# Layer 0's border in another order, two key tiles beside an attention's first items, and weight chunks split inside the work ahead of them

## The chip, the cores and the metric

One core of a Trainium2 chip runs the whole program in one launch. The metric is device time in microseconds. The kernel before took 1628.4 us (median of three runs, 1627.59 to 1629.45).

## What is computed

Two blocks of two layers each, fp32, width D = 1024, one sequence x of 256 tokens; the second block has a context ctx of 256 tokens beside it. The part that the change touches, cut:

```python
# first block: h = layer_norm(DN_ALPHA*h + mixer(h)), a pooling mixer, then a dilated attention whose
# keys and values come from h @ w_kv; its result h is the x of the second block.
def rms_norm(x, g): return x * rsqrt(mean(x*x) + EPS) * g
for l in range(2):                          # second block
    sh1, sc1, g1, sh2, sc2, g2 = split(silu(c) @ w_mod[l] + b_mod[l], 6)     # for x, and the same for ctx
    h_x, h_c = [rms_norm(v, norm_g[l, 0]) * (1 + sc1) + sh1 for v in (x, ctx)]
    if l == 0:   # even mixer, on x and ctx
        qa, ka, va, qb, kb, vb = split_cols(h @ w_in[l], EVEN_SPLITS)
        qa, ka = rms_norm(qa, qk_g[0]), rms_norm(ka, qk_g[1])                # 8 query heads, 2 key heads of 64
        # x's q and k get a rotary embedding; x attends to ctx and x, ctx to ctx
        o_a = softmax(qa @ ka.T) @ va
        lam = exp(sum(lam_p[0]*lam_p[1])) - exp(sum(lam_p[2]*lam_p[3])) + lam0
        o_b = rms_norm((softmax(qb1 @ kb1.T) - lam * softmax(qb2 @ kb2.T)) @ vb, subln_g) * (1 - lam0)
    else:        # odd mixer: windowed attention C with a sink, neighbourhood attention D with the bias rpb
        o_a, o_b = windowed_attend(...), neighborhood_attend(..., rpb)
    x = x + g1 * rms_norm(concat(o_a, o_b) @ w_out[l], norm_g[l, 1])
    h2 = rms_norm(x, norm_g[l, 2]) * (1 + sc2) + sh2
    x = x + g2 * rms_norm(square(relu(h2 @ w_mlp_in[l])) @ w_mlp_out[l], norm_g[l, 3])
    # ctx gets the same two updates in layer 0
```

## The kernel before

**Weights.** All weights come as one stream of 210 chunks of 1 MB (128 x 2048) through three `raw` slots, issued by SP (SyncE). A matrix product is made of three fp32r products (`mm3`, L548 to L550): high half by high, low by high, high by low. So each chunk is split: ACT (ScalarE) copies its high half into `whi` (`split_hi`, L1014), DVE (VectorE) subtracts it into `wlo` (`split_lo`, L1024). There are four split slots, and ACT waits before chunk w until the unit of chunk w − 4 is `used` up by PE (TensorE). A unit is one weight block, such as q2, k2, v2 (the projections of the second block), out, in and out of the MLP. `split_to(name)` on ACT and on DVE splits all chunks up to the end of that unit and ahead of it, as far as slots allow; with a second argument 0 only up to its end; `last_split` (L996) works out which chunk that is. The features (activations, token or feature on the partitions) are split in the same way, into `fhi` by ACT (L1069) and `flo` by DVE or POOL (L1556, L2243).

**Order.** Each engine's program is written out by hand. An instruction gives a label by `did(...)`, and another engine waits by `after(...)`; an engine goes strictly in order, so what stands behind a waiting instruction waits with it. PSUM's banks are handed out in turn by `job(...)` on PE, which waits until the bank's last user has been `read` by ACT or DVE.

**Tiles.** Token tiles 0 and 1 are x, 2 and 3 are ctx, each of 128 tokens. `by_token` (L562) projects tiles of tokens with a unit; q2 is 512 columns wide, k2 256 (two key heads and two value heads). `turn_normed` transposes normed tiles into features (L600), with `modulate` (DVE or POOL) making h * (1 + scale) + shift on the way.

**The border between the blocks.** The last projection of the first block is unit outb, in two halves of one unit each, for x's tiles 0 and 1. DVE adds the residual (`add_residual`), takes `statistics` and `moments`, ACT takes the `root` of the variance, DVE the `gain_shift` (layer norm). Then ACT squares the tile (`squares`) and takes the root for the second block's rms norm (`stream_root`, L1325), and DVE norms it (`normed`, L1929 to L1937). The ctx tiles need only the latter. ACT's list is at L1355 to L1373, DVE's at L2097 to L2140, PE's in the branch for l == 0 near L919. After it, PE goes q2 of ctx, k2 of ctx, transposes of x, q2 of x, heads of ctx turned, k2 of x, attention.

**Attentions.** Each attention is a list of items; an item is the scores of one head and one tile of queries (L682, L690), DVE's maximum (L1764), ACT's exponential, PE's transposes of the probabilities (L724) and the product with the values (L752). Work that has no part in them is set between the items as side steps, pairs of (item, step): `side_steps_pairs` for the second attention of layer 0, the differential one (16 items), `side_steps_halves` for its first. Every engine runs through the same list in `attend` (PE L755, ACT L1237, DVE L1850) and does its share of a step. Head norms are made by `head_squares` (ACT, L1390), `head_sums` (DVE, L2020 to L2029), `head_roots`, `head_scaled`, and `turn_heads` (PE).

**The first block's attention** has DVE's two instructions for lam (L1923 and L1924) in front of its items; they wait for ACT's exponential of the sums (L1297).

**MLP of layer 0.** `hidden(0, j)` on ACT and `square_hidden` on DVE make the hidden features of in-unit j, for the first two units with ctx and x apart; `mlp_out` on PE multiplies with out-unit j later. Between layers stand `residual` (L1967), `stream_root` and `normed` again.

**Layer 1.** `split_to(("k2", 1, 0), 0)`, the wait for the DMAs of the odd mixer's tables (`loads["odd"]`, L2121) and `modulate(("n1", 1, 1), ...)` follow each other on DVE. POOL adds the rpb rows to the column mask, one instruction for each of the bias loads (L2298).

## Time and profile before

| | |
|---|---|
| median of three runs | 1628.4 us (1627.59 to 1629.45) |
| the profiled execution: its own time, its span | 1627.03 us, 1625.2 us |
| PE busy (matmuls; weight loads beside them) | 1531.4 us, 94% of the span (1307.4 us, 80%) |
| DVE busy | 872.8 us, 54% |
| ACT busy | 677.1 us, 42% |
| POOL busy | 152.6 us, 9% |
| TensorE clock granted, mean | 0.977 of full speed |
| DMA | 233.89 MB, mean 144 GB/s |

The span is the time from the first to the last instruction of one execution. PE busy is the union of its matmuls; its ends are modelled, so a busy PE need not be at its peak. Under half clock, the same matmuls take about twice the time and PE counts as busy all the same.

### The profile page before, as it was taken

What the parts mean: (1) busy time and instruction counts of PE and PEld (TensorE: products, weight loads), DVE (VectorE), ACT (ScalarE), POOL (GpSimd) and SP (SyncE); (2) the same over time, 40 slices, a digit from 0 to 9 for tenths busy, and PEclk for the clock granted to TensorE, in tenths of its full rate; (3) what the DMA queues carried; (4) which work ended last, traced back from release to release, by engine and by line L of the source; (5) the groups of instructions that cost most, each with busy time, mean ns of one, the idle gap of its engine ahead of it and who ended that gap; (6) DMA issues with size and microseconds to landing.
All of it is one profiled execution on the core that took longest, in us unless ns stands there. A gap on an engine that the chain in (4) does not pass through costs nothing.

```text
span 1625.2 us, 24158 instructions
## 1 busy us (share of the span) xinstructions
PE 1531.4 (94%) x9546; PEld 1307.4 (80%) x9546; DVE 872.8 (54%) x1505; ACT 677.1 (42%) x1096; POOL 152.6 (9%) x119
## 2 busy tenths in 40 slices
PE   7999899999999979998998999999998999979998
PEld 7998798999997756785797777777786777779887
DVE  6786654545546765347574343333457455655444
ACT  5454344544435335336454122232235335544443
POOL 2100310000000110000013001111002020020110
PEclk9999999999999979999999999999999999989999
DMA  6455655353536315220231453543512421145451
GB/s 247 173 200 208 231 209 198 138 182 131 182 106 231 135 52 208 104 87 18 78 130 53 156 188 135 195 183 134 201 52 94 134 71 53 69 166 188 175 194 66
DMA packets 43770, 233.89 MB, mean 144 GB/s; under 512 B 13136, under 2 KB 14224, under 8 KB 16784
## 3 DMA queue, kind: packets, MB, share of 16 engines
q1 hardware_dynamic: 31232, 222.38, 36.8%
q10 hardware_dynamic: 12432, 10.01, 2.2%
q8 instruction: 77, 1.26, 0.3%
q14 instruction: 29, 0.24, 0.0%
HBM read 231.29 MB, written 1.08 MB: 143 GB/s over the span
## 4 chain that ended last, share of the span: by engine, by line
PE 84%; DVE 8%; ACT 4%; issue 2%; POOL 1%; DMA 0%; ACTq 0%; DVEq 0%; SPq 0%
PE ps L548 23%; PE ps L550 23%; PE ps L549 23%; PE ps L752 5%; PE ps L638 3%; DVE wlo L1024 3%; PE ps L724 3%; PE ps L690 2%; ACT whi L1014 2%; PE ps L682 1%; PE ps L600 1%; DVE nmax L1764 1%; POOL flo L2243 1%; PE ps L622 1%; ACT fhi L1069 0%
## 5 line engine op out<-in xcount | busy, mean ns | idle before, releaser
L1024 DVE TENSOR_TENSOR wlo<-raw,whi 128x2048 fp32r<-128x2048 f32 x162 | 383.5, 2392 | 282.9 <-ACT whi L1014 282.7
L548 PE MATMUL ps<-fhi,whi 128*128 128x256 f32 (+1 forms) x1280 | 393.3, 307 | 13.6 <-DVE wlo L1024 7.1
L1014 ACT ACTIVATE whi<-raw 128x2048 fp32r<-128x2048 f32 x162 | 304.0, 1906 | 224.3 <-PE ps L550 168.7
L549 PE MATMUL ps<-flo,whi 128*128 128x256 f32 (+1 forms) x1280 | 389.3, 304 | 0.0
L550 PE MATMUL ps<-fhi,wlo 128*128 128x256 f32 (+1 forms) x1280 | 389.3, 304 | 0.0
L548 PEld LDWEIGHTS ps<-fhi,whi 128*128 128x128 f32 x1280 | 247.3, 193 | 37.3 <-issue 9.5
L549 PEld LDWEIGHTS ps<-flo,whi 128*128 128x128 f32 x1280 | 247.2, 193 | 8.9
L550 PEld LDWEIGHTS ps<-fhi,wlo 128*128 128x128 f32 x1280 | 247.0, 193 | 9.0
L548 PE MATMUL ps<-whi,fhi 128*128 128x512 f32 (+1 forms) x592 | 209.6, 354 | 14.3 <-DVE mix L2029 5.4
L549 PE MATMUL ps<-wlo,fhi 128*128 128x512 f32 (+1 forms) x592 | 206.1, 348 | 0.0
L550 PE MATMUL ps<-whi,flo 128*128 128x512 f32 (+1 forms) x592 | 206.1, 348 | 0.0
L548 PE MATMUL ps<-whi,hhi 128*128 128x512 f32 x384 | 153.2, 399 | 7.8 <-issue 7.8
L550 PE MATMUL ps<-whi,hlo 128*128 128x512 f32 x384 | 152.2, 396 | 0.0
L549 PE MATMUL ps<-wlo,hhi 128*128 128x512 f32 x384 | 152.2, 396 | 0.0
L548 PEld LDWEIGHTS ps<-whi,fhi 128*128 128x128 f32 x592 | 114.8, 194 | 33.0 <-issue 6.6
L550 PEld LDWEIGHTS ps<-whi,flo 128*128 128x128 f32 x592 | 114.6, 194 | 13.6
L549 PEld LDWEIGHTS ps<-wlo,fhi 128*128 128x128 f32 x592 | 114.9, 194 | 12.7
L1992 DVE TENSOR_TENSOR htmp<-htmp 128x256 f32<-128x256 f32 (+1 forms) x72 | 47.1, 654 | 116.3 <-ACT htmp L1349 116.3
L2254 POOL TENSOR_TENSOR hlo<-htmp,hhi 128x256 fp32r<-128x256 f32 (+1 forms) x72 | 66.4, 922 | 439.3 <-ACT hhi L1354 439.3
L548 PEld LDWEIGHTS ps<-whi,hhi 128*128 128x128 f32 x384 | 72.5, 189 | 29.1 <-issue 12.1
L550 PEld LDWEIGHTS ps<-whi,hlo 128*128 128x128 f32 x384 | 72.3, 188 | 17.6
L549 PEld LDWEIGHTS ps<-wlo,hhi 128*128 128x128 f32 x384 | 72.5, 189 | 17.0
(238 smaller groups left out, 1784.4 us busy)
## 6 DMA issues: line engine op xcount, KB each, us to landing
raw<-in_wstream SPq DMA_DIRECT2D x210, 1024.0 KB, 5.0
gates<-gated ACTq DMA_DIRECT2D x6, 512.0 KB, 4.3
hx<-in_x SPq DMA_DIRECT2D x1, 1024.0 KB, 5.1
lnrow<-in_ln_g ACTq DMA_DIRECT2D x2, 512.0 KB, 4.1
lnrow<-in_ln_b ACTq DMA_DIRECT2D x2, 512.0 KB, 5.3
hc<-in_ctx ACTq DMA_DIRECT2D x1, 1024.0 KB, 6.0
mix<-in_rpb_rows ACTq DMA_DIRECT2D x4, 256.0 KB, 5.1
hc<-in_rpb_rows ACTq DMA_DIRECT2D x4, 256.0 KB, 3.9
```

The source lines that it names most:

```text
L548: mm(o, lh, rh, start=start, stop=False)
L549: mm(o, lh, rl, start=False, stop=False)
L550: return mm(o, ll, rh, start=False, stop=stop)
L600: ins = nc.tensor.transpose(o[:, c:c + P], src(t)[:, k * P:k * P + P], ident[:, :])
L638: ins = mm(o[at:at + 32, :], condz[:, 2 * k:2 * k + 32], raw[:, c % RAW_SLOTS, base:base + NW], start=k < 4, stop=k >= 4, tile_position=(0 ...
L690: ins = mm(o, QT[l][po:po + DH, tq, q0 + t * P:q0 + t * P + P], KT[l][po:po + DH, tk, k0:k1], start=True, stop=True)
L724: ins = nc.tensor.transpose(o[:, (j - b) * P:(j - b + 1) * P], e[:, i % 3, j * P:j * P + P], ident[:, :])
L752: ins = mm(o[:, 0:dv], p[:, i % 2, j * P:j * P + P], v, start=j == 0, stop=j == kt - 1)
L1014: nc.scalar.activation(whi[:, w % SPLIT_SLOTS, :], raw[:, c % RAW_SLOTS, :], ACT.Copy).then_inc(*did("scalar", ("hi", w)))
L1024: nc.vector.tensor_tensor(wlo[:, w % SPLIT_SLOTS, :], raw[:, c % RAW_SLOTS, :], whi[:, w % SPLIT_SLOTS, :].bitcast(F32), ALU.subtract).the ...
L1992: v.tensor_tensor(h, h, h, ALU.mult).then_inc(*did("vector", ("squared",) + key))
L2254: p.tensor_tensor(hlo[:, j % 2, e, cols], htmp[:, e % 2, cols], hhi[:, j % 2, e, cols].bitcast(F32), ALU.subtract).then_inc(*did("pool", * ...
```

## The change

Eight places are edited. Lambda's two DVE instructions move from the first block's attention to layer 0's border. In the border, ACT's root for ctx comes before the features and weights, chunks for outb and q2 are split as their slots come free, and PE's order becomes k2 of one ctx tile, transposes of x, k2 of the other, q2 of tile 0, heads of ctx, q2 of tile 1. k2 of x's tiles becomes the side step "keys" of items 0 and 1 of the attention that follows; one chunk is split before that attention and one, the step "ahead", at item 2; roots, scalings and turns come one item later. In layer 0's second attention, the transposes of the mixed ctx tiles ("fo") go from items 13 and 14 to 15 and 16. In the MLP, the chunks of out-unit 0 are split between the last two groups of hidden tiles. At the border to layer 1, k2's chunk is split ahead of the norm, the residual has one label for each tile so that ACT squares a tile behind its own, and modulate goes ahead of the wait for the tables. POOL's bias add is made in four quarters.

```diff
--- before.py
+++ after.py
...
@@ -433,7 +433,7 @@
         return None
-    if step[0] in ("chunk", "bias", "mod", "fo", "weights", "roots", "scaled", "turn"):
+    if step[0] in ("chunk", "bias", "mod", "fo", "weights", "roots", "scaled", "turn", "keys", "ahead"):
         return None
...
@@ -447,7 +447,7 @@
-    return [(1, ("v2", 0, 1, 0)), (3, ("v2", 0, 1, 1)), (12, ("weights",))] + [(13 + j // 2, ("fo", j)) for j in range(4)]
+    return [(1, ("v2", 0, 1, 0)), (3, ("v2", 0, 1, 1)), (12, ("weights",))] + [(15 + j // 2, ("fo", j)) for j in range(4)]
...
@@ -463,9 +463,10 @@
-    return [(2, ("roots",)), (3, ("scaled", "q", 0)), (4, ("scaled", "k", 0)), (5, ("scaled", "q", 1)),
-            (6, ("scaled", "k", 1)), (7, ("turn", "q", 0)), (8, ("turn", "k", 0)), (9, ("turn", "q", 1)),
-            (10, ("turn", "k", 1))]
+    return [(0, ("keys", 0)), (1, ("keys", 1)), (3, ("roots",)),
+            (2, ("ahead", PLACE[UNIT["q2", 0, 1].w0] + 1)),
+            (4, ("scaled", "q", 0)), (5, ("scaled", "k", 0)), (6, ("scaled", "q", 1)), (7, ("scaled", "k", 1)),
+            (8, ("turn", "q", 0)), (9, ("turn", "k", 0)), (10, ("turn", "q", 1)), (11, ("turn", "k", 1))]
...
@@ -764,11 +765,15 @@
             for at, step in steps:
-                if step[0] in ("chunk", "bias", "weights", "roots", "scaled"):
+                if step[0] in ("chunk", "bias", "weights", "roots", "scaled", "ahead"):
                     continue
...
                         turn_heads(step[1], 0, [step[2]], 4 if step[1] == "q" else 2)
+                    continue
+                if step[0] == "keys":
+                    if at == i:
+                        by_token(UNIT["k2", 0, 0], ("k2", 0, 0), [step[1]], width=256, first=False, last=step[1] == 1)
                     continue
...
@@ -919,12 +924,13 @@
                 by_token(UNIT["q2", 0, 0], ("q2", 0, 0), (2, 3), feat=("n1", 0, 1), last=False)
-                by_token(UNIT["k2", 0, 0], ("k2", 0, 0), (2, 3), width=256, last=False)
+                by_token(UNIT["k2", 0, 0], ("k2", 0, 0), [2], width=256, last=False)
                 turn_normed(0, 0, 0)
-                by_token(UNIT["q2", 0, 0], ("q2", 0, 0), (0, 1), feat=("n1", 0, 0), first=False)
+                by_token(UNIT["k2", 0, 0], ("k2", 0, 0), [3], width=256, first=False, last=False)
+                by_token(UNIT["q2", 0, 0], ("q2", 0, 0), [0], feat=("n1", 0, 0), first=False, last=False)
                 turn_heads("q", 0, (2, 3), 4)
                 turn_heads("k", 0, (2, 3), 2)
-                by_token(UNIT["k2", 0, 0], ("k2", 0, 0), (0, 1), width=256, first=False)
+                by_token(UNIT["q2", 0, 0], ("q2", 0, 0), [1], first=False)
             else:
...
@@ -1250,6 +1256,12 @@
                     continue
+                if step[0] in ("keys", "ahead"):
+                    if at == i and step[0] == "keys":
+                        head_squares("k", step[1])
+                    elif at == i:
+                        split_hi(act, step[1], st)
+                    continue
                 if at == i and step[0] == "bias":
...
@@ -1323,12 +1335,12 @@
     def stream_root(l, which, group):
-        if which or l:
-            act.wait_ge(*after("resid", *((l, 0) if which else (0, 1)), group))
-        elif group != (2, 3):
+        if not which and not l and group != (2, 3):
             act.wait_ge(*after("ln", 1, group[0]))
...
             for t in group:
+                if which or l:
+                    act.wait_ge(*after("resid", *((l, 0) if which else (0, 1)), t))
                 squares(("sq", l, which, t), t)
...
@@ -1357,17 +1369,18 @@
         squares(("sq", 0, 0, t), t)
+    stream_root(0, 0, (2, 3))
     split_features("fo1", 0)
     split_to(("outb", 0))
-    stream_root(0, 0, (2, 3))
     split_features(("n1", 0, 1), 1, (0, 0))
     for t in range(XT):
-        if t:
-            split_to(("outb", 1))
-            split_to(("k2", 0, 0), 0)
         act.wait_ge(*after("var", 1, t))
         root(rstd[:, t:t + 1], mv[:, t, 1:2], 1, 1, "root", "ln", 1, t)
+        if t == 0:
+            split_to(("outb", 1))
         stream_root(0, 0, (t,))
+        if t == 0:
+            split_to(("k2", 0, 0), 0)
...
@@ -1407,7 +1420,6 @@
             if l == 1:
-                split_to(("k2", 1, 0), 0)
                 split_features(("n1", 1, 1), 1, (1, 0))
...
@@ -1415,14 +1427,12 @@
                     head_squares("k", t)
-                for t in (0, 1):
-                    head_squares("q", t)
+                split_hi(act, PLACE[UNIT["q2", 0, 1].w0], st)
+                head_squares("q", 0)
                 for what in "qk":
...
                         turned(what, 0, t)
-                split_to(("k2", 0, 0))
-                for t in (0, 1):
-                    head_squares("k", t)
+                head_squares("q", 1)
             elif part == 0:
...
@@ -1483,6 +1493,7 @@
             hidden(0, 0, 0)
+            split_to(("out", 0, 0), 0)
             hidden(0, 1, 0)
...
@@ -1500,8 +1511,9 @@
             mixer_root(0, 1, (2, 3))
+            split_to(("k2", 1, 0), 0)
             stream_root(1, 0, (2, 3))
-            act.wait_ge(*after("resid", 0, 1, (2, 3)))
+            act.wait_ge(*after("resid", 0, 1, 3))
             act.wait_ge(*after("split", ("n1", 1, 0), 3))
...
@@ -1866,6 +1878,10 @@
                     low_feature(("fo", 0, 1), 1, step[1])
+                if at == i and step[0] == "keys":
+                    head_sums("k", step[1])
+                if at == i and step[0] == "ahead":
+                    split_lo(step[1], st)
                 if at == i and step[0] == "roots":
...
@@ -1919,10 +1935,6 @@
                                  heads_view(qkg[:, i, 16 * (1 - half):], (0, 2), (32, 2), (1, 16)), ALU.mult))
-    dve.wait_ge(*after("lam exp"))
-    link(v.tensor_tensor(lam[:, 2:3], lam[:, 1:2], lam[:, 0:1], ALU.subtract))
-    link(v.tensor_scalar(lam[:, 3:4], lam[:, 2:3], -LAM0, None, ALU.add))
-
     items = items_first()
...
@@ -1971,7 +1983,7 @@
                 dve.wait_ge(*after("gated half", l, which, t, n))
-            labels = [("resid", l, which, group)] if t == group[-1] else []
+            labels = [("resid", l, which, t)]
             if l and which:
...
@@ -2095,46 +2107,50 @@
         if l == 0:
+            mod_columns(0, 0)
             low_features("fo1", 0)
-            mod_columns(0, 0)
             normed(0, 0, (2, 3))
-            for t in range(XT):
-                if t:
-                    split_to(("outb", 1))
-                else:
-                    split_to(("outb", 0))
-                for n in range(2):
-                    if n == 0:
-                        dve.wait_ge(*after("h1", t))
-                    add_residual("outb", n, t)
-                    statistics("outb", n, t)
-                    if (t, n) == (0, 0):
-                        modulate(("n1", 0, 1), 0, 0, 1)
-                moments(1, t)
-                gain_shift(t)
-                if t:
-                    split_to(("k2", 0, 0), 0)
-                normed(0, 0, (t,))
+            split_to(("outb", 0))
+            dve.wait_ge(*after("h1", 0))
+            add_residual("outb", 0, 0)
+            statistics("outb", 0, 0)
+            modulate(("n1", 0, 1), 0, 0, 1)
+            add_residual("outb", 1, 0)
+            statistics("outb", 1, 0)
+            moments(1, 0)
+            gain_shift(0)
+            dve.wait_ge(*after("h1", 1))
+            add_residual("outb", 0, 1)
+            statistics("outb", 0, 1)
+            split_to(("outb", 1))
+            normed(0, 0, (0,))
+            add_residual("outb", 1, 1)
+            statistics("outb", 1, 1)
+            moments(1, 1)
+            gain_shift(1)
+            split_to(("k2", 0, 0), 0)
+            normed(0, 0, (1,))
+            dve.wait_ge(*after("lam exp"))
+            link(v.tensor_tensor(lam[:, 2:3], lam[:, 1:2], lam[:, 0:1], ALU.subtract))
+            link(v.tensor_scalar(lam[:, 3:4], lam[:, 2:3], -LAM0, None, ALU.add))
             modulate(("n1", 0, 0), 0, 0, 0, before=("n1", 0, 1))
-        else:
+        if l == 1:
+            modulate(("n1", 1, 1), 1, 0, 1)
             dve.wait_ge(loads["odd"], 48)
             link(v.tensor_scalar(nsink[:, :], sinkr[:, :], -1.0, None, ALU.mult))
-        if l == 1:
-            split_to(("k2", 1, 0), 0)
-            modulate(("n1", 1, 1), 1, 0, 1)
         if l == 0:
-            for g in (1, 0):
-                for what in "qk":
-                    for t in (2 * g, 2 * g + 1):
-                        head_sums(what, t)
-                if g:
-                    head_roots(1)
-                    for what in "qk":
-                        for t in (2, 3):
-                            head_scaled(what, t)
+            for what in "qk":
+                for t in (2, 3):
+                    head_sums(what, t)
+            head_roots(1)
+            for what in "qk":
+                for t in (2, 3):
+                    head_scaled(what, t)
+            split_lo(PLACE[UNIT["q2", 0, 1].w0], st)
+            for t in (0, 1):
+                head_sums("q", t)
             dve.wait_ge(loads["late"], 32)
             link(v.tensor_scalar(sublng[:, :], sublng[:, :], 1.0 - LAM0, None, ALU.mult))
-            split_to(("k2", 0, 0))
             items = items_second(0, 0)
...
@@ -2176,6 +2192,7 @@
             square_hidden(0, 0, 0)
+            split_to(("out", 0, 0), 0)
             square_hidden(0, 1, 0)
...
@@ -2203,6 +2220,7 @@
             residual(0, 1, (2, 3))
+            split_to(("k2", 1, 0), 0)
             normed(1, 0, (2, 3))
...
@@ -2295,8 +2313,9 @@
         rows = b.rearrange("p t (h c) -> p (t h) c", c=S)
-        p.tensor_tensor(rows, rows, heads_view(colmask, (0, 8), (1, S)), ALU.add).then_inc(
-            *did("pool", *([("bias",)] if n else [])))
+        for h in range(0, 8, 2):
+            p.tensor_tensor(rows[:, h:h + 2, :], rows[:, h:h + 2, :], heads_view(colmask, (0, 2), (1, S)), ALU.add).then_inc(
+                *did("pool", *([("bias",)] if n and h == 6 else [])))
     low_modulated(("n2", 1, 0), 1, 1, 0)
...
```

## Rows read from the trace of the kernel before

**Rows 1.** The chain of waits that ended last, shares of the span by engine

```profile
PE 84%; DVE 8%; ACT 4%; issue 2%; POOL 1%; DMA 0%; ACTq 0%; DVEq 0%; SPq 0%
```

**Rows 2.** Timeline, first attention: start us, length us, engine, line, operation, [idle before <-releaser]

```profile
265.11 1.56 PE L682 MATMUL ps<-kq 64*128 64x256 f32 x12
...
267.99 0.16 DVE L1923 TENSOR_TENSOR lam<-lam 128x1 f32<-128x1 f32 x1 [5.11 <-ACT lam L1297]
...
275.42 0.58 PE L548 MATMUL ps<-fhi,whi 128*128 128x256 f32 x1 [2.80 <-ACT kq L1213]
```

**Rows 3.** Stretches: window, us, busy of PE, PEld, DVE, ACT, POOL, clock, DMA, GB/s

```profile
275.40:281.60 6.20, 6.18 (x29) 6.18 (x30) 5.78 (x7) 2.69 (x4) 0.00 (x0) 0.51 0.75 280
...
573.80:578.50 4.70, 4.70 (x11) 3.73 (x12) 4.18 (x18) 0.45 (x3) 0.66 (x1) 0.51 0.00 0
...
601.50:609.60 8.10, 7.94 (x35) 3.87 (x35) 5.44 (x22) 3.40 (x13) 0.00 (x0) 0.53 0.51 192
...
889.40:893.00 3.60, 3.60 (x10) 2.86 (x11) 2.06 (x1) 0.97 (x1) 0.00 (x0) 0.58 1.00 403
```

**Rows 4.** Timeline, layer 0's border, first half

```profile
517.54 2.07 ACT L1069 ACTIVATE fhi<-ps 128x512 fp32r<-128x512 f32 x4 [0.93 <-PE ps L600]
...
523.22 1.28 ACT L1143 ACT_TABLE_LOAD   x1
...
527.27 3.55 PE L600 MATMUL ps<-ident,mix 128*128 128x128 f32 x16 [2.54 <-DVE mix L1937]
...
549.45 0.47 PE L548 MATMUL ps<-whi,fhi 128*128 128x512 f32 x1 [2.27 <-issue]
```

**Rows 5.** Timeline, layer 0's border, second half, PE

```profile
560.65 0.36 PE L548 MATMUL ps<-whi,fhi 128*128 128x256 f32 x1
...
566.48 1.91 PE L600 MATMUL ps<-ident,mix 128*128 128x128 f32 x16
...
573.80 0.79 PE L548 MATMUL ps<-whi,fhi 128*128 128x512 f32 x1 [5.42 <-DVE mix L2029]
```

**Rows 6.** Timeline, opening of layer 0's first attention

```profile
587.78 0.69 DVE L2027 TENSOR_REDUCE hss<-mix 128x8 f32<-128x512 f32 x1 [2.64 <-ACT mix L1397]
...
594.10 1.14 PE L690 MATMUL ps<-kT,qT 64*128 64x256 f32 x8
...
596.05 4.49 DVE L1024 TENSOR_TENSOR wlo<-raw,whi 128x2048 fp32r<-128x2048 f32 x2
...
601.53 0.69 PE L724 MATMUL ps<-ident,e 128*128 128x128 f32 x2 [6.30 <-ACT e L1166]
...
610.31 0.70 PE L690 MATMUL ps<-kT,qT 64*128 64x256 f32 x4
```

**Rows 7.** Timeline, end of layer 0's second attention

```profile
768.50 0.87 PE L600 MATMUL ps<-ident,mix 128*128 128x128 f32 x3 [4.63 <-DVE mix L1846]
...
773.79 1.29 DVE L1556 TENSOR_TENSOR flo<-ps,fhi 128x512 fp32r<-128x512 f32 x2 [2.86 <-ACT fhi L1069]
```

**Rows 8.** Timeline, MLP of layer 0, first out-unit

```profile
882.84 5.49 ACT L1014 ACTIVATE whi<-raw 128x2048 fp32r<-128x2048 f32 x3
...
884.76 6.69 DVE L1024 TENSOR_TENSOR wlo<-raw,whi 128x2048 fp32r<-128x2048 f32 x3 [2.28 <-ACT whi L1014]
...
889.36 0.76 PE L548 MATMUL ps<-whi,hhi 128*128 128x512 f32 x1 [7.75 <-issue]
```

**Rows 9.** Timeline, border of layer 1

```profile
1244.65 0.17 DVE L2121 TENSOR_SCALAR nsink<-sinkr 128x8 f32<-128x8 f32 x1 [1.38 <-DMA band<-in_t_band]
...
1247.29 0.46 PE L548 MATMUL ps<-whi,fhi 128*128 128x256 f32 x1 [1.94 <-DVE wlo L1024]
...
1258.52 0.58 PE L548 MATMUL ps<-whi,fhi 128*128 128x256 f32 x1 [3.76 <-DVE e_b L2084]
```

**Rows 10.** Timeline, last attention: POOL's bias add and a DVE instruction beside it

```profile
1323.72 6.09 POOL L2298 TENSOR_TENSOR mix<-mix 128x2048 f32<-128x2048 f32 x1 [69.25 <-DMA hc<-in_rpb_rows]
...
1326.31 3.52 DVE L1799 TENSOR_TENSOR nmax<-nmax,nsink 128x1 f32<-128x1 f32 x1
```

## The prediction

> **What bounds the kernel now.** I began with the chain of waits that ended last: 84% of it is PE [rows 1]. So a microsecond is worth something only where PE stands idle or runs at half clock, and I listed PE's idle stretches of over one microsecond in its timeline. The reader should look at two things in such a row: the number in brackets (how long PE had been idle) and the engine behind the arrow. Beside it stands the granted clock of the stretch behind the gap. It has two levels, 1.00 (2.4 GHz) and 0.50 (1.2 GHz), and after four of the gaps here it was about 0.5 for 3 to 10 us [rows 3], though PE was then busy nearly all the time. So a gap costs its length and something behind it. Eight of the gaps lie where the diff edits: at the first attention's opening, three at layer 0's border, one at the opening of its first attention, one in its second, one in its MLP and three at the border of layer 1.
>
> **The change, part by part.** All times are of the profiled execution: span 1625.2 us, its own time 1627.0, while the median of the three runs is 1628.4, 1.4 above it. I make the sum against 1627.0 and add the 1.4.
>
> *1. Lambda out of the way of the first attention.* The DVE instruction at 267.99 had waited 5.11 us for ACT's exponential of lam, and the first item's maximum stands two short instructions behind it, at 268.4, although its scores ended at 266.67 (265.11 + 1.56) [rows 2]. The two instructions go to layer 0's border, where they cost 0.4 us in DVE's stream before the last modulate. The maximum, the exp and what ACT does behind it (two weight splits, then the copies of k) move up by 1.7. PE's gap of 2.80 at 275.42 is ended by those copies [rows 2], so it shrinks to 1.1. Behind it, the clock was 0.51 for 6.2 us [rows 3]: 3.1 us of full-rate work lost. With so short a gap I expect most of that back, but not for certain. Value 3.6; bounds 1.5 (clock stays down) and 4.5.
>
> *2. Layer 0's border, first half.* PE's gap of 2.54 at 527.27 waited for DVE's normed ctx tiles, and the 16 transposes there took 3.55 us where the same 16 took 1.91 at 566.48 [rows 4, 5]. DVE in turn waited for the root, which ACT ran behind two weight splits, the table load at 523.22 being its first part [rows 4]. Now the root stands directly behind the two squares, near 516.6. That puts 1.28 (load) + 0.3 (root) ahead of the first attention's features; ACT had 0.93 idle before them [rows 4], so PE starts the outb projection 0.65 later and then runs through: 2.54 + 1.64 − 0.65 = 3.5 gained.
> The Trainium skill ("ScalarE: Activation LUTs", What ACT_TABLE_LOAD costs) gives 2.66 us for a switch of sets, a drain of 1.38 included. By it this part would gain 1.4 less. In the trace the load took 1.28 and the root began right behind it; the sum uses that.
> The next gap, 2.27 at 549.45 [rows 4], is q2's weights: ACT split them only behind tile 0's square and root, DVE behind tile 0's norm. Now both split them as soon as the slots are free, ahead of that. By my replay the low half of the first chunk lands 0.4 after PE gets there: 1.9 gained. On the other side, k2's chunk is split between tile 1's statistics and its norm, and by the same replay PE waits 0.4 for it. Together 3.5 + 1.9 − 0.4 = 5.0; bounds 3.0 and 5.8.
>
> *3. Border, second half.* The gap of 5.42 at 573.80 lay between the transposes of x's normed tiles and q2 of tile 0 [rows 5]. From the first transpose (566.48) to 573.80 are 7.3 us, and this chain (modulate on DVE, copy on ACT, low half on POOL, then DVE's first reading of q2's tile 2, which frees the bank) is unchanged. But k2 of tile 3 now stands inside it: two k2 tiles take 566.48 − 560.65 = 5.8 [rows 5], so one fills 2.9, and the gap falls to 2.5. Behind the old gap the clock was 0.51 for 4.7 us [rows 3], 2.3 lost. Behind the 2.54 of part 2 the transposes ran at half rate too [rows 4], so a gap of this size can bring it; I take 1.6 of the 2.3. Value 2.9 + 1.6 = 4.5; bounds 2.9 and 5.2.
>
> *4. Opening of the attention over ctx and x.* Before, all of q2 and k2 came first, then PE stood still for 6.30 us at 601.53 while DVE did the sums of two k2 tiles and 4.49 us of weight splits at 596.05 before the first maximum; the clock then was 0.53 for 8.1 us [rows 3, 6]. From the end of the projections (594.10, where the first scores begin) to the scores of items 6 and 7 (610.31) are 16.2 us [rows 6]. Now k2's x tiles (2 × 2.9) are done by PE at items 0 and 1, one chunk is split before the attention and the other, the step "ahead", at item 2. Replayed with the rows' durations: DVE's sums of q2's tile 1, of four instructions like that at 587.78 [rows 6], follow the projection with ACT's square ahead of them; the first maximum starts 3.7 after it; then DVE and ACT take turns (maximum, exp, squares, sums) for items 0 to 2, and at item 2 ACT splits 1.9 and DVE 2.3, each waiting for the other. The probabilities' copy of item 0 stands behind ACT's split, so PE idles about 4 us there and 1.5 more at item 1's, and reaches the scores of items 6 and 7 some 18.7 after the projections. Of these, 5.8 are work that stood before the 594.1: 16.2 − (18.7 − 5.8) = 3.3 gained at full clock. A gap of 4 will bring half clock again; as its first part falls into waiting, I charge 1.5. Queued behind the added waits are, on DVE, the roots and the maxima of items 3 and later, and on ACT every exp. From item 7 on PE is busy nearly all the time in this attention, and the later roots, scalings and turns (one item later than before) lie beside it. Value 1.8; bounds −3 (the taking of turns longer by two 2.3-us splits) and 3.5.
>
> *5. Second attention of layer 0.* PE waited 4.63 us at 768.50 for the end of DVE's norm of the ctx pairs, as the transposes of the mixed tiles came at item 13 [rows 7]. Worse, they made DVE wait for ACT's copies of them, 2.86 at 773.79 [rows 7], in a stretch where DVE sets the pace. Now they come at items 15 and 16. PE's gap does not go, it waits for item 12's probabilities instead; but DVE no longer idles: by replay, 3.6 us until the last probabilities. Bounds 2.5 and 4.2.
>
> *6. MLP of layer 0.* PE idled 7.75 us at 889.36, at the first product with w_mlp_out. ACT had split nothing until 882.84, behind all 16 half-width hidden tiles, and DVE's low halves came from 884.76 [rows 8]. Now the first two chunks are split before the last four hidden tiles. Their slots are free when PE ends its last product with the first "in" unit, four half-width products of 2.9 (as a k2 tile [rows 5]) before it went idle at 881.6: at 870. ACT and DVE need 3.7 and 4.5 us, done by about 878, before the 881.6. The four hidden tiles come later by up to 5 us, but PE needs them only a unit later. All 7.75 go, and the half clock behind it (0.58 for 3.6 us [rows 3]) gives 1.5 to 2.0 more. Value 9.6; bounds 7.7 and 10.
>
> *7. Border of layer 1.* DVE stood 1.38 at 1244.65 for a DMA, then did k2's low half, and PE waited 1.94 for that at 1247.29; the modulate stood behind both, and PE's 3.76 at 1258.52 hangs on it through the split and DVE's first reading of q2 [rows 9]. Now k2's split is ahead of the norm, the square of each tile follows its own residual, and modulate is ahead of the DMA wait. Modulate moves from 1247.1, behind that low half, to about 1243.8 and so does all behind it: 3.2, with the clock behind the gap unsettled. Value 3.0; bounds 1.5 and 3.5.
>
> *8. POOL's bias adds in quarters.* A DVE instruction of 0.16 us took 3.52 at 1326.31, while POOL's add of 6.09 ran [rows 10]. The quarters shorten such a block, but PE had projections to do meanwhile: 0; bounds −0.3 and 0.5.
> The Trainium skill ("SBUF — State Buffer", Who interferes with whom) says that a DVE instruction with two SBUF inputs and a GpSimd one hold a shared port pair each for its whole length, which these rows agree with. It also lets the loser be POOL. That changes nothing in the sum.
>
> Sum: 3.6 + 5.0 + 4.5 + 1.8 + 3.6 + 9.6 + 3.0 = 31.1. 1627.0 − 31.1 = 1595.9, and with the 1.4, 1597.3.
>
> **The rivals.** *A: the opening eats the border.* DVE and ACT serve items 0 to 3 alone and in turn; if part 4 goes to its bound and the clock stays at half behind parts 1, 3 and 4, 5 + 2 + 1.6 + 1.5 are missing: about 1607. For it speaks that all of the opening's stall was DVE's work even before [rows 6], and that DVE now gets more of it there; against it, that PE has 5.8 us of keys to do there.
> *B: the clock comes back everywhere.* Gains at the upper bounds of 1 to 4 and 6: about 1592.
> *C: nothing much.* The gains would have to be returned by a later bound, weights above all. No gap of PE in the rows is put down to a weight transfer, so little speaks for it: 1626 to 1630.
> *D: slower.* The clock is the one mechanism that can cost this much: with the small gaps spread where there were few large ones, PE could be held at 1.2 GHz through the long products. To undo 31 us it takes 62 us more at half clock than now; with 80 us more, 1637. Against it: in each half-clock stretch PE had been idle just before, and the change leaves fewer such places.
>
> **How the numbers follow.** Forecast as worked out (1591 to 1603): 0.68. A: 0.20. B: 0.08. C: 0.02. D: 0.02. The predicted time is the forecast's, 1597. For 8 in 10, the range takes in nearly all of A and the inner part of B: 1591 to 1609. A measurement here tells about 0.2%, 3.3 us, from no change: faster 0.96, same 0.02, slower 0.02.
>
> **What would show it.** PE's timeline: no gap before the first product with w_mlp_out (part 6); none of over 1 us before the transposes of the ctx tiles and before q2 in the border (part 2); the gap before q2 of tile 0 near 2.5 (part 3); first probabilities' transposes without 6 us before them but a gap of about 4 before item 0's values (part 4); DVE without the 2.86 wait in the second attention (part 5); no wait for lam (part 1); k2 of layer 1 directly behind its transposes (part 7). The prediction is wrong if PE's idle time merely moves to items 0 to 8 of the attention, or if the half-clock stretches grow longer than those they replace.

## The result

The changed kernel takes 1600.8 us (median of four runs, 1599.48 to 1601.32), the kernel before 1628.0 beside it; the ratio is 0.9831, 95% interval 0.9818 to 0.9843. That is 27.2 us less, where 31.1 had been forecast. In the two profiled executions the spans are 1625.2 and 1599.5, 25.7 apart: that of before was 1.0 under its median (1627.0), that of the changed kernel 0.5 above (1601.3).

The page of the changed kernel: its span, the busy rows, and the chain that ended last, by engine [rows 1].

```profile
span 1599.5 us, 24162 instructions
PE 1525.6 (95%) x9546; PEld 1301.0 (81%) x9546; DVE 867.3 (54%) x1505; ACT 677.1 (42%) x1096; POOL 153.8 (10%) x125
...
PE 83%; DVE 10%; ACT 3%; issue 2%; POOL 1%; DMA 0%; ACTq 0%; DVEq 0%; SPq 0%
```

PE does the same 9546 products in 5.8 us less busy time; the rest of the gain is idle time that went. Where it went is read from PE's timeline after, at the places of the prediction (start us, length us, engine, line, operation, [idle before <-releaser]; the lines of the changed file are 1 to 18 higher):

```profile
275.12 0.38 PE L549 MATMUL ps<-fhi,whi 128*128 128x256 f32 x1 [1.21 <-ACT kq L1219]
...
522.13 1.91 PE L601 MATMUL ps<-ident,mix 128*128 128x128 f32 x16
...
540.82 0.47 PE L549 MATMUL ps<-whi,fhi 128*128 128x512 f32 x1 [0.42 <-issue]
...
562.61 0.50 PE L549 MATMUL ps<-whi,fhi 128*128 128x512 f32 x1 [2.67 <-DVE mix L2041]
...
588.58 1.08 PE L753 MATMUL ps<-vv,p 128*128 128x64 f32 x4 [4.08 <-ACT p L1191]
...
592.85 3.64 PE L639 MATMUL ps<-raw,condz 128*32 128x512 f32 x16
597.52 0.70 PE L691 MATMUL ps<-kT,qT 64*128 64x256 f32 x4
...
600.33 0.66 PE L753 MATMUL ps<-vv,p 128*128 128x64 f32 x4 [1.11 <-DVE modrow L1700]
...
758.81 1.12 PE L725 MATMUL ps<-ident,e 128*128 128x128 f32 x4 [4.28 <-DVE e L1824]
...
868.32 0.39 PE L549 MATMUL ps<-whi,hhi 128*128 128x512 f32 x1
...
1220.70 1.94 PE L601 MATMUL ps<-ident,mix 128*128 128x128 f32 x16 [1.53 <-DVE mix L1949]
...
1232.94 0.58 PE L549 MATMUL ps<-whi,fhi 128*128 128x256 f32 x1 [4.55 <-DVE e_b L2096]
```

Against [rows 2, 4 to 9]: 2.80 became 1.21, the 2.54 before the ctx transposes is gone (they take 1.91 again), the 2.27 before q2 0.42, the 5.42 before q2 of tile 0 2.67, and the 7.75 before w_mlp_out is gone. The 6.30 at the attention's opening became a 4.08 in another place, the 4.63 of the pairs a 4.28. At layer 1's border the 1.94 is gone and the 3.76 became a 4.55: PE reaches it 3.7 us earlier than before, counted from the transposes (1232.94 − 4.55 − 1220.70 = 7.7, before 1258.52 − 3.76 − 1243.41 = 11.4), DVE's reading that ends it comes 2.9 earlier.

How much each part brought is read as PE's lead over the kernel before, at the same instruction in both timelines (where the order changed, at the end of the same piece of work):

| between | lead at its end, us | part | measured | forecast |
|---|---|---|---|---|
| start and the first block's second layer (185.23, 186.06) | −0.8 | none | −0.8 | 0 |
| ... and the end of that attention (512.34, 509.29) | 3.05 | 1 | 3.9 | 3.6 |
| ... and q2's first product (549.45, 540.82) | 8.6 | 2 | 5.6 | 5.0 |
| ... and the end of q2 of x (588.2, 576.6) | 11.55 | 3 | 2.9 | 4.5 |
| ... and item 12 of the attention (635.72, 623.80) | 11.9 | 4 | 0.4 | 1.8 |
| ... and out2 of ctx behind the second attention (798.53, 785.42) | 13.1 | 5 | 1.2 | 3.6 |
| ... and the second out-unit (913.31, 890.82) | 22.5 | 6 | 9.4 | 9.6 |
| ... and layer 1's first attention (1270.65, 1245.06) | 25.6 | 7 | 3.1 | 3.0 |
| ... and the end | 25.7 | 8 | 0.1 | 0 |

The first line is not the change's: over the traces here the first block's second layer began anywhere from 185.2 to 187.7. The stretches behind it repeat far better. From the scores at 266.40 to those at 283.94, all twelve traces with the new place of lambda have 17.54 or 17.55 us; from there to the first scores of layer 0's attention, the seven with this border, its gap unfilled, and the key tiles beside the items have 292.57 to 292.86.

The granted clock behind the gaps (window, us, busy of PE, PEld, DVE, ACT, POOL, clock, DMA share, GB/s):

```profile
275.10:281.00 5.90, 5.88 (x49) 5.88 (x50) 5.77 (x7) 2.49 (x4) 0.00 (x0) 1.00 0.75 271
562.60:569.90 7.30, 7.29 (x26) 5.84 (x27) 6.78 (x22) 2.25 (x4) 0.65 (x1) 0.77 0.00 0
588.60:597.20 8.60, 8.20 (x34) 3.97 (x35) 6.57 (x21) 2.29 (x9) 0.00 (x0) 0.50 0.48 149
758.80:765.10 6.30, 6.29 (x26) 4.56 (x27) 4.09 (x11) 2.26 (x7) 0.00 (x0) 0.55 0.00 0
1232.90:1237.00 4.10, 4.06 (x19) 4.07 (x20) 4.05 (x6) 0.25 (x2) 0.00 (x0) 0.50 0.59 240
```

Of these five, the clock is back only behind the gap of 1.21. The reader should put the second and fourth rows beside parts 3 and 5 of the table: these are the two parts that came out short with their gap at about the forecast place.

### The profile page after: what moved, and what is told of

The parts are those of the page before. It is cut to its first block, busy times and chain, and to the rows that moved or that the text cites. A ratio compares the mean times of both kernels' runs of the same rounds, so it can differ in the third digit from the quotient of the medians.

```text
span 1599.5 us, 24162 instructions
## 1 busy us (share of the span) xinstructions
PE 1525.6 (95%) x9546; PEld 1301.0 (81%) x9546; DVE 867.3 (54%) x1505; ACT 677.1 (42%) x1096; POOL 153.8 (10%) x125
## 3 DMA queue, kind: packets, MB, share of 16 engines
HBM read 231.29 MB, written 1.08 MB: 145 GB/s over the span
## 4 chain that ended last, share of the span: by engine, by line
PE 83%; DVE 10%; ACT 3%; issue 2%; POOL 1%; DMA 0%; ACTq 0%; DVEq 0%; SPq 0%
PE ps L549 23%; PE ps L551 22%; PE ps L550 22%; PE ps L753 5%; DVE wlo L1030 3%; PE ps L639 3%; PE ps L725 3%; PE ps L691 2%; PE ps L683 2%; ACT whi L1020 1%; POOL flo L2261 1%; PE ps L601 1%; DVE nmax L1776 1%; PE ps L623 1%; ACT fhi L1075 0%
## 5 line engine op out<-in xcount | busy, mean ns | idle before, releaser
L549 PE MATMUL ps<-fhi,whi 128*128 128x256 f32 (+1 forms) x1280 | 391.9, 306 | 11.9 <-DVE wlo L1030 7.1
```

The source lines that it names most:

```text
L549: mm(o, lh, rh, start=start, stop=False)
```

## The experiments

All are edits of the changed kernel unless said otherwise; none leaves out any work. They are read in two ways: by the median, and by stretches of PE's timeline between the same instructions, which leaves out the spread of the start. The border's first half and PE's new order in it (parts 2 and 3) were not undone in a run of their own; what they brought is read from the timelines alone.

**1. The transposes of the mixed tiles back at items 13 and 14.**

```diff
-    return [(1, ("v2", 0, 1, 0)), (3, ("v2", 0, 1, 1)), (12, ("weights",))] + [(15 + j // 2, ("fo", j)) for j in range(4)]
+    return [(1, ("v2", 0, 1, 0)), (3, ("v2", 0, 1, 1)), (12, ("weights",))] + [(13 + j // 2, ("fo", j)) for j in range(4)]
```

> The changed kernel with the transposes of the mixed ctx tiles back at items 13 and 14. In the two traces the second attention of layer 0 gained 1.2 us between the same two places of PE's stream (11.9 us ahead before it, 13.1 behind it), where the prediction had 3.6. Theory 1 (the order does what it does in the traces): 1.2 us slower than the changed kernel, 1602.0. Theory 2 (the prediction's 3.6 is there, and something else in the changed kernel took 2.4 of it back): 3.6 slower, 1604.4. Theory 3 (the order is worth nothing by itself): the same, 1600.8.

1602.0 us (1599.52 to 1602.22), 1.2 slower. From item 12 of the first attention to layer 1's transposes its timeline has 598.1 us against 596.9. Theory 1: the new order is worth 1.2, not 3.6. The medians alone would not show it (the four runs of each overlap), the traces do: from item 12 to the ctx transposes behind the attention it has 161.14, as before the change (161.15), and the seven traces with the new order and no extra transposes in the pairs' gap have 159.54 to 160.03.

**2. The key tiles and both chunks ahead of the attention**, with the old side steps, on the new border.

```diff
-    return [(0, ("keys", 0)), (1, ("keys", 1)), (3, ("roots",)),
-            (2, ("ahead", PLACE[UNIT["q2", 0, 1].w0] + 1)), ...
+    return [(2, ("roots",)), (3, ("scaled", "q", 0)), ...
```

> The changed kernel with its new border, but the two key tiles of x and both weight chunks ahead of the attention again, and roots, scalings and turns at the old items. The prediction gave the opening 1.8 us; the two traces give it 0.4 (11.55 us ahead at the end of the q2 tiles, 11.92 behind the first items). Theory 1 (traces): 0.4 slower than the changed kernel, 1601.2. Theory 2 (the prediction's sum): 1.8 slower, 1602.6. Theory 3 (the opening eats, DVE and ACT in turn): faster, 1598 or less.

1597.7 us (1597.32 to 1597.98), 3.1 faster: theory 3. Moving the keys into the items lost time; the opening as a whole still came out 0.4 ahead because the border now splits one of the two chunks beforehand: ahead of the first maximum DVE has one split of 2.29 here, where it had 4.49 of them before. DVE's rows show the difference, first here, then in the changed kernel:

```profile
583.96 2.29 DVE L1030 TENSOR_TENSOR wlo<-raw,whi 128x2048 fp32r<-128x2048 f32 x1
586.16 1.08 DVE L1779 TENSOR_REDUCE nmax<-ps 128x1 f32<-128x256 f32 x3
```

```profile
580.34 0.42 DVE L1776 TENSOR_REDUCE nmax<-ps 128x1 f32<-128x256 f32 x1
581.73 0.29 DVE L2039 TENSOR_REDUCE hss<-e 128x2 f32<-128x128 f32 x1 [0.97 <-ACT e L1410]
...
582.85 0.41 DVE L1776 TENSOR_REDUCE nmax<-ps 128x1 f32<-128x256 f32 x1
584.23 0.29 DVE L2039 TENSOR_REDUCE hss<-subtmp 128x2 f32<-128x128 f32 x1 [0.97 <-ACT subtmp L1410]
...
585.35 0.41 DVE L1776 TENSOR_REDUCE nmax<-ps 128x1 f32<-128x256 f32 x1
588.19 2.29 DVE L1030 TENSOR_TENSOR wlo<-raw,whi 128x2048 fp32r<-128x2048 f32 x1 [2.43 <-ACT whi L1020]
```

With the keys done, three maxima take 1.08 us together; with the keys between them they come 2.5 us apart: between two of them DVE waits 0.97 for ACT's square, which stands behind an exp that waited for the maximum, and then does the keys' sum and rotation.

**3. Work for PE in the pairs' gap.** PE makes transposes of the identity into a free PSUM bank; nobody reads them. All other instructions and their order stay, so what can change is the clock.

```diff
+    def fill(n, skip=0):
+        b = state["banks"][(turn[0] + skip) % len(state["banks"])]
+        if b in last:
+            pe.wait_ge(*after("read", *last[b]))
+        for c in range(n):
+            nc.tensor.transpose(ps[:, b, c % 4 * P:c % 4 * P + P], ident[:, :], ident[:, :])
...
+    if items[0][0] == "B" and i == 14:
+        fill(34)
     if 0 <= i - 2 < len(items):
         turns(i - 2, items[i - 2])
```

> The changed kernel; PE makes 34 transposes that nobody reads (some 4.0 us) into a free PSUM bank at item 14 of layer 0's second attention, where it stands idle 4.28 us; behind that gap the clock was 0.55 for 6.3 us, and DVE then waited 2.11 us for scores. Theory 1 (the part that the prediction missed there is the half clock behind the gap): clock near 1.0 behind it, the wait of 2.11 nearly gone, up to 2.2 us faster than the changed kernel, 1598.6 to 1599.3. Theory 2 (it is the order of PE's queue and DVE's pace): the clock may rise, the time stays, 1600.8.

1598.0 us (1596.84 to 1599.09), 2.8 faster; counted from item 12, layer 1's transposes come 2.6 earlier than in the changed kernel's timeline. PE's rows in the pairs and the clock of the same stretch:

```profile
754.30 3.93 PE L554 MATMUL ps<-ident 128*128 128x128 f32 x34
...
758.65 0.66 PE L734 MATMUL ps<-ident,e 128*128 128x128 f32 x4 [0.42 <-DVE e L1835]
...
760.13 1.13 PE L700 MATMUL ps<-kT,qT 64*128 64x512 f32 x4
```

```profile
758.00:762.00 4.00, 3.58 (x26) 2.47 (x24) 3.93 (x10) 3.00 (x9) 0.00 (x0) 1.00 0.00 0
```

In the changed kernel the same scores took 2.08 and DVE waited for them:

```profile
763.69 1.29 DVE L1776 TENSOR_REDUCE nmax<-ps 128x1 f32<-128x512 f32 x2 [2.11 <-PE ps L691]
```

With the clock up this wait is gone: DVE's three maxima follow each other without idle time at 756.20, 758.77 and 761.34. Theory 1.

**4. The same in three gaps** (20 transposes at the border, 32 ahead of item 0's values).

```diff
     by_token(UNIT["k2", 0, 0], ("k2", 0, 0), [3], width=256, first=False, last=False)
+    fill(20, 3)
     by_token(UNIT["q2", 0, 0], ("q2", 0, 0), [0], feat=("n1", 0, 0), first=False, last=False)
...
+    if items[0][0] == "A" and i == 3:
+        fill(32)
     if 0 <= i - 3 < len(items):
         values(i - 3, items[i - 3])
```

> The same, and idle transposes in two more gaps of PE: 32 ahead of item 0's values in the first attention of layer 0 (gap 4.08, then clock 0.50 for 8.6 us), and 20 ahead of q2 of tile 0 in the border (gap 2.68, then 0.77 over 7.3 us). Theory 1 (half clock is what the border and the opening gave back): 1.6 at the border, 2.6 at the opening (what DVE waits for the scores of items 6 and 7) and up to 2.2 at the pairs: 1594.4 to 1596. Theory 2 (DVE and ACT set the pace in all three): 1599 to 1601.

1597.4 us (1595.93 to 1598.55), where theory 1 had 1594.4 to 1596. The border gave what it should: clock 1.00 over 562 to 570, and the first scores 300.06 us after the first attention's products, against 301.51, so 1.45 gained (the seven traces with this gap unfilled lie within 0.3 of each other). Behind the opening 0.9 of it was left (324.33 against 325.21 to the values behind the gap of 1.11):

```profile
590.27 1.08 PE L762 MATMUL ps<-vv,p 128*128 128x64 f32 x4 [1.63 <-ACT p L1205]
...
590.00:597.00 7.00, 6.73 (x30) 3.28 (x30) 3.75 (x16) 1.92 (x7) 0.00 (x0) 0.51 0.78 270
```

With the 4.08 filled, PE ran into the next gap, 1.63, and the half clock came behind that one. So at the border and the pairs the clock was what was lost. At the opening the transposes moved the half clock and did not remove it, and so the run does not tell whether DVE and ACT set the pace there (theory 2) or the clock.

**5. The chunk at item 8 in place of 2.**

```diff
-            (2, ("ahead", PLACE[UNIT["q2", 0, 1].w0] + 1)),
+            (8, ("ahead", PLACE[UNIT["q2", 0, 1].w0] + 1)),
```

> The changed kernel with the step ahead (one weight chunk, 1.9 us of ACT and 2.3 of DVE) at item 8 in place of item 2; the key tiles stay at items 0 and 1. The run with keys and chunks in front of the attention was 3.1 us shorter between the same two places of PE's stream (967.99 before, 945.58 changed, 942.47). Theory 1 (what the opening loses is the chunk, which stands between item 0's probabilities and item 3's maximum): the gap of 4.08 us ahead of item 0's values falls below 1.5, the half clock behind it goes, 1597 to 1598. Theory 2 (it is the keys, since ACT and DVE take turns between exp, squares, sums and maximum for items 0 to 2): under 1 us better, 1600 to 1601.

1611.3 us (1609.28 to 1612.46), 10.5 slower: both theories miss. Up to item 5's values it was 3.0 ahead of the changed kernel, though PE still idled 2.29 ahead of item 0's values, with the clock at 0.57 behind it; then:

```profile
602.95 0.63 PE L753 MATMUL ps<-vv,p 128*128 128x64 f32 x4 [2.12 <-ACT p L1191]
605.44 1.23 PE L691 MATMUL ps<-kT,qT 64*128 64x256 f32 x4 [1.87 <-ACT e L1172]
609.47 1.94 PE L639 MATMUL ps<-raw,condz 128*32 128x512 f32 x8 [0.90 <-DMA raw<-in_wstream]
613.11 1.93 PE L639 MATMUL ps<-raw,condz 128*32 128x512 f32 x8 [1.71 <-DMA raw<-in_wstream]
```

In stretches (the last three figures are the clock, the DMA share and GB/s):

```profile
592.00:600.00 8.00, 6.89 (x47) 3.92 (x39) 3.74 (x12) 2.39 (x8) 0.00 (x0) 0.84 0.00 1
600.00:610.00 10.00, 5.11 (x28) 3.44 (x31) 4.12 (x9) 5.08 (x12) 0.00 (x0) 0.74 0.44 162
610.00:620.00 10.00, 8.29 (x39) 4.46 (x31) 2.00 (x8) 1.95 (x6) 0.00 (x0) 0.50 0.90 359
```

An unsplit chunk keeps its `raw` slot, and SP loads the stream in order: from 592 to 600 the DMA share is 0.00. PE then waited twice for weights, and half clock followed. The step at item 2 is there for the stream, which my prediction had not weighed.

**6. Lambda back in front of the first attention.**

```diff
+    dve.wait_ge(*after("lam exp"))
+    link(v.tensor_tensor(lam[:, 2:3], ...)); link(v.tensor_scalar(lam[:, 3:4], ...))
     items = items_first()
     attend(items, [], side_steps())
...
     normed(0, 0, (1,))
-    dve.wait_ge(*after("lam exp"))
-    link(v.tensor_tensor(lam[:, 2:3], ...)); link(v.tensor_scalar(lam[:, 3:4], ...))
     modulate(("n1", 0, 0), 0, 0, 0, before=("n1", 0, 1))
```

> The changed kernel with lambda's two instructions in front of the first attention again. Theory 1 (prediction, part 1: 1.7 of gap and most of 3.1 of half clock): 3.6 to 3.9 us slower than the changed kernel, 1604.5, with a gap of 2.80 ahead of the second projection group and clock about 0.5 for 6 us behind it. Theory 2 (only the wait moves, the clock is another matter): 1.6 slower, 1602.4.

1605.6 us (1602.52 to 1606.63), 4.8 slower. The gap is as expected, 2.74 at 277.85, but in the profiled execution the clock behind it stayed up, and this execution was 1.6 late at the first block's second layer already. So the wait's 1.5 (2.74 less 1.21) is shown by the trace; the clock's share is not a fixed sum, and the runs of this kernel spread over 4.1 us. Another 1.6 came in this execution between the first scores and item 12 of layer 0's attention (48.74 against 47.17), at a place that the edit does not touch. The median's 4.8 is above both theories, and why is not shown:

```profile
277.80:283.80 6.00, 5.95 (x49) 5.95 (x50) 5.81 (x7) 2.58 (x4) 0.00 (x0) 1.00 0.71 273
```

**7. The out-unit's chunks split behind the hidden tiles.**

```diff
     hidden(0, 0, 0)
-    split_to(("out", 0, 0), 0)
     hidden(0, 1, 0)
...
     square_hidden(0, 0, 0)
-    split_to(("out", 0, 0), 0)
     square_hidden(0, 1, 0)
```

> The changed kernel with the chunks of the first out-unit split behind the last hidden tiles again. Theory 1 (prediction, part 6): 9.4 to 9.6 us slower, 1610.2, PE idle 7.75 us ahead of the first product with w_mlp_out. Theory 2 (the earlier weights let later stages run ahead as well or take something back there): over 10.5 or under 8.5.

1611.1 us (1609.81 to 1611.65), 10.3 slower; by the timeline, pairs to layer 1, 9.9 (460.15 against 450.26). The gap is back, 7.75 at 876.10, with clock 0.50 behind it. Theory 1 in kind: 0.3 above its range by the timeline, 0.7 by the medians.

**8. Layer 1's border and POOL's adds as before.**

```diff
     mixer_root(0, 1, (2, 3))
-    split_to(("k2", 1, 0), 0)
     stream_root(1, 0, (2, 3))
...
-    labels = [("resid", l, which, t)]
+    labels = [("resid", l, which, group)] if t == group[-1] else []
...
-    modulate(("n1", 1, 1), 1, 0, 1)
     dve.wait_ge(loads["odd"], 48)
     link(v.tensor_scalar(nsink[:, :], sinkr[:, :], -1.0, None, ALU.mult))
+    split_to(("k2", 1, 0), 0)
+    modulate(("n1", 1, 1), 1, 0, 1)
...
-    for h in range(0, 8, 2):
-        p.tensor_tensor(rows[:, h:h + 2, :], rows[:, h:h + 2, :], heads_view(colmask, (0, 2), (1, S)), ALU.add)
+    p.tensor_tensor(rows, rows, heads_view(colmask, (0, 8), (1, S)), ALU.add)
```

> The changed kernel with layer 1's border as before (k2's chunk split behind the norm, one residual label for each pair of tiles, modulate behind the wait for the tables) and POOL's bias adds whole. The two places lie 60 us apart in the trace and are read apart. Theory 1 (prediction, parts 7 and 8): 3.0 us slower at the border, 0 to 0.3 behind it: 1603.8 to 1604.1. Theory 2 (the gap of 3.76 stood for a wait of its own, and its end hangs on something that the edit does not move): 1.5 or less at the border, 1602.3.

1604.9 us (1604.41 to 1605.03), 4.1 slower. Border: 39.96 us from its transposes to item 0's values against 37.00, so 3.0. POOL's part: 112.89 us in the attention behind it against 112.59, so 0.3. Theory 1.

**9. Transposes in nine gaps**, on the kernel of experiment 2.

```diff
     turn_features("fx", ...)
+    fill(40)
...
+    fill(38)
     turn_features("f1", ...)
...
+    if items[0][0] == "A" and i == 2:
+        fill(33)                            # pairs 34 and border 20 as above
...
+    fill(36, 2)
     by_token(u, ("k2", l, 0), (2, 3), width=256, feat=("n1", l, 1), first=False)
...
+    if items[0][0] == "C" and i == 8:
+        fill(28, 4)
...
+    fill(68)
     turn_normed(1, 1, 0)
...
+    fill(26)
     for j in range(9):
```

> The kernel with keys and chunks ahead of the attention (1597.7), and transposes that nobody reads in nine gaps of PE: 40 at the start (4.81), 38 ahead of the transposes between the first block's layers (4.53), 20 at layer 0's border (2.67), 33 ahead of item 0's probabilities (4.10), 34 at the pairs (4.28), 36 at layer 1's border (4.57), 28 in the last attention (3.73), 68 and 26 at the last norm (8.48 and 3.42). The half clock behind them costs at most, as the granted clock of the stretches shows: 2.8 + 2.4 + 1.5 + 3.0 + 2.6 + 3.0 + 2.4 + 1.6 + 1.6 = 20.9 us. Theory 1 (the half clock behind a gap is lost work wherever PE has a long run of products behind it): all but about 2 us of the attention's share comes back, 1577 to 1581. Theory 2 (it is lost only where the runs so far showed it, at the border and at the pairs, 4.1 together; elsewhere DVE and ACT set the pace): 1593 to 1594.

1600.3 us (1598.4 to 1601.88), though the mean clock rose from 0.982 to 0.992. Both theories miss, for three reasons that PE's timeline shows:

```profile
1232.58 0.41 PE L925 MATMUL ps<-ident,e_b 128*128 128x128 f32 x2 [1.23 <-DVE e_b L2125]
...
1279.98 4.32 PE L553 MATMUL ps<-ident 128*128 128x128 f32 x19 [5.54 <-ACT p_b L1212]
...
1407.28 4.70 PE L553 MATMUL ps<-ident 128*128 128x128 f32 x26 [4.21 <-DVE htmp L1612]
```

In the last two the bank that they were given was itself being waited for, so they stood in the way: the last attention took 117.90 us against 112.43 in experiment 2, and the stretch behind it 225.20 against 222.70, in spite of what the 68 gained there. At layer 1's border they did what they should, and k2 of ctx was done sooner; but DVE was at two weight splits (4.49 us), PE waited 1.23 for it, and the half clock (0.50 over 1234 to 1238) came behind that wait: 38.35 us against 36.76, 1.6 lost. At the start they were worth 0.

**10. Keys at items 0 and 1, both chunks ahead of the attention.**

```diff
-            (2, ("ahead", PLACE[UNIT["q2", 0, 1].w0] + 1)),
...
     head_squares("q", 1)
+    split_hi(act, PLACE[UNIT["q2", 0, 1].w0] + 1, st)
...
     for t in (0, 1):
         head_sums("q", t)
+    split_lo(PLACE[UNIT["q2", 0, 1].w0] + 1, st)
```

> The changed kernel with the key tiles at items 0 and 1 as they are, but the second weight chunk split ahead of the attention too, with no step at item 2. With keys and chunks both ahead of the attention, the same stretch was 3.1 us shorter; with the chunk at item 8 it was 3.0 us shorter up to item 5's values and then lost 13 us, PE waiting for weight transfers. Theory 1 (the chunk's place at item 2 is what costs, and the keys beside the items cost nothing): 2.5 to 3.5 faster than the changed kernel, 1597.3 to 1598.3. Theory 2 (the keys' taking of turns costs as well): 0 to 1.5 faster, 1599.3 to 1600.8.

1599.8 us (1597.67 to 1601.69), 1.0 faster; from the first attention's products to item 12, 348.07 us against 348.68, 0.6. Experiment 2 has 345.97. So of its 2.7 in this stretch 0.6 are the chunk's place at item 2 and 2.1 the keys': theory 2. The medians say the same of the keys (1599.8 against 1597.7); the 0.6 is smaller than the spread of this opening in other pairs of traces (1.6 in experiment 6), and is not shown. The split itself costs more than its place: without it anywhere near (experiment 5) item 5's values came 2.4 earlier than here.

**11 and 12. Six gaps and seven**, on experiment 2, without the three that cost time or gave nothing; number 11 gives the last in-unit's transposes a bank that is already its own, and 12 adds 28 in the last attention, into a bank of the side projections.

```diff
-    fill(40)
-    fill(36, 2)
-    fill(28, 4)
+    fill(28, side=1)                        # number 12 alone
-    fill(26)
+    fill(24, bank=counts.banks[("acc", 0, 0)])
```

> As the kernel with transposes in nine gaps, less the three that the traces showed to be worth nothing or to cost time (start: 0; layer 1's border: products end earlier, PE then waits 1.23 and 0.51 for DVE and the half clock comes behind that, 1.6 lost; last attention and last in-unit: the bank that the transposes were given was itself being waited for, about 9.5 lost together). Left are 38, 20, 33, 34, 68, and 24 ahead of the last in-unit into a bank that waits for nothing. Theory 1: against keys and chunks ahead (1597.7), 0.4 + 2.4 (border and opening) + 2.2 to 2.6 + 0.7 + 1.6 = 7.3 to 7.7: 1590.0 to 1590.4. Theory 2 (what the transposes gain early is taken back by a later wait, as at layer 1's border): 1593 or more.

> The same with 28 transposes more in the last attention's gap of 3.73 us, this time into a bank of the side projections. Behind the gap the clock was 0.50 for 2.7 us and 0.74 for 4.0 us, 2.4 us of full-rate work lost. Theory 1 (PE has 24 products behind the scores, so the clock counts): 1.5 to 2.4 faster than the one with six, 1588 to 1588.8. Theory 2 (DVE's chunk of 2.29 us sets the pace here, and the bank is not free in time): 0 or slower, 1590.3 and more.

1591.3 us (1590.3 to 1593.88) and 1590.2 us (1590.08 to 1591.25); ratios to the kernel before 0.977 (0.9757 to 0.9783) and 0.9763 (0.975 to 0.9777). Theory 1 in number 11, about 1 above its range. The seventh gave 1.1 by the medians and 1.4 by the timeline (111.84 against 110.40 in the last attention), just under theory 1's range. The unfilled attention took 111.84 to 113.36 in twelve traces, so 1.4 is the least that it can be. The traces also show what theory 1's sum had wrong: against experiment 2, 0.5 came between the first block's layers, 1.45 at the border, 2.2 at the pairs and 2.1 at the last norm, but from the first scores to item 12 the two took 40.87 and 39.45, and experiment 2, without transposes, 38.68. A gain from the 33 at the opening is not shown. Both are faster than either kernel of this case, by 9.5 and 10.6 us against the changed one.

## Why the prediction was right, and where it was off

The time lay in the range, 3.5 us above the forecast and with the sign as forecast.

That is not luck in the main, as five parts of eight were right one by one. But 5.4 us are missing in parts 3 to 5, and the 0.9 that parts 1 and 2 gave beyond their values took some of it back.

**Parts 1, 2, 6, 7 and 8** came within 0.6 us of their values. The working held, down to the details: PE started the outb projection behind a gap of 0.83 where it had been 0.20, so 0.63 later, and the working had 0.65; the mechanism of part 2, root ahead of the splits, and of part 6, splits ahead of four hidden tiles, is what the rows show. PE's wait for k2's chunk (0.23, worked out as 0.4) belongs to part 2 and lies in part 3's line of the table. In part 1 the clock gave 2.6, more than the 1.9 counted on. It is read from the first product behind the gap (275.42, 275.12) to the next scores, before and after:

```profile
286.86 1.57 PE L682 MATMUL ps<-kq 64*128 64x128 f32 x12
```

```profile
283.94 1.57 PE L683 MATMUL ps<-kq 64*128 64x128 f32 x12
```

That is 11.4 us and 8.8. With 1.6 of idle time the place itself gave 4.2, of which the table's longer stretch shows 3.9. A slip without weight: the gaps where the diff edits, counted out in the same sentence, are ten and not eight.

**Part 3, 2.9 for 4.5.** The gap was placed right (2.67 for 2.5). The step that failed is "I take 1.6 of the 2.3": the clock gave back 0.3. Behind the smaller gap it was still 0.77 over 7.3 us. Experiment 4, with the clock at 1.00 there and the rest as it was, brought 1.45, about what was missing; experiments 9, 11 and 12 have the same 1.45 against experiment 2.

**Part 4, 0.4 for 1.8.** Two terms failed. The first is "I charge 1.5" for half clock: it held for 8.6 us, over the sixteen products of the modulation that took 3.64, and the scores of items 6 and 7 came 20.9 us after the projections (597.52 − 576.63), where the replay's 18.7 and the 1.5 make 20.2. So at that point 1.2 was gained, counted from the start of k2 of x before (588.2). The second stood at nothing, "the later roots, scalings and turns lie beside it": from those scores to item 12 the changed kernel took 26.3 us and the one before 25.4, with a gap of 1.11 for DVE at 600.33, where the one before had 0.72. Rival A's mechanism, DVE and ACT in turn, was at work inside the part, at a price of 2.1 for the keys (experiments 2 and 10). It was in the replay too, but the prediction set no sum beside it for keys left ahead of the attention, and that order was the faster one. A's 1607 needed some 10 us missing in parts 1, 3 and 4; 3.0 were, in parts 3 and 4.

**Part 5, 1.2 for 3.6.** The step that failed is "but DVE no longer idles". PE's gap of 4.28 brought half clock, for which this part had no term; item 15's scores, behind item 12's transposes and values in PE's queue, ended late, and DVE waited 2.11 for them. ACT's copies still made it wait 1.63 more at 767.99. Experiment 3, which leaves all but the clock there as it was, brings 2.6, about the missing 2.4.

**Part 7, 3.1 for 3.0.** The sum is right by its mechanism: modulate moved up by 3.2, as worked out. The clock behind PE's last gap there, which it left unsettled, did not come back: 0.50 behind the 4.55 as behind the 3.76 before (1258.5 to 1264).

**The rivals.** B (the clock back everywhere) is ruled out by the windows. C and D did not happen; D's mechanism, small gaps that hold the clock down, shows in experiments 4 and 9, where it cost 0.6 and 1.6 us.

Open: what the clock is worth in part 1 on the average. Between the two traces it was 2.6; the trace of experiment 6 had the gap and not the half clock, and its median the full 4.8.

## What to carry to other kernels

Cost a gap of PE with its length and, as a term of its own, with the half clock behind it, also where the gap only moves: here two parts were short by that term and a third in part. Where PE is needed at once behind a gap and nobody else sets the pace, transposes that nobody reads, into a bank that is surely free, gave 1.4 to 2.6 us a gap at the border, the pairs and the last attention; at the opening and at layer 1's border another engine was late next, and a gap with half clock behind it came one wait later, so read who would be late next before filling. Don't put a step that needs two engines in turn between an attention's first items, and before a weight split is delayed look at what its buffer holds up.
